# A hybrid transformer block with expert retrieval on one core: GpSimd builds the gated one-hots as outer products of two short factors, and 32 instead of 24 groups are scattered beside the routing

## What the block computes

```python
def peer_ffn(h, w_query, sub_keys, expert_u, expert_v):
    q = (x @ w_query).reshape(T, PEER_HEADS, 2, PEER_HALF)
    s1 = jnp.einsum('thd,kd->thk', q[:, :, 0], sk[0])
    s2 = jnp.einsum('thd,kd->thk', q[:, :, 1], sk[1])
    v1, i1 = lax.top_k(s1, PEER_TOPK)
    v2, i2 = lax.top_k(s2, PEER_TOPK)
    cand = (v1[..., :, None] + v2[..., None, :]).reshape(T, PEER_HEADS, PEER_TOPK * PEER_TOPK)
    sc, flat = lax.top_k(cand, PEER_TOPK)
    e = (jnp.take_along_axis(i1, flat // PEER_TOPK, axis=-1) * PEER_NKEYS
         + jnp.take_along_axis(i2, flat % PEER_TOPK, axis=-1))
    g = jax.nn.softmax(sc, axis=-1).astype(h.dtype)
    ...
        u = expert_u[ec]
        a = jax.nn.gelu(jnp.einsum('cd,chkd->chk', xc, u))
        return jnp.einsum('chk,chkd->cd', gc * a, expert_v[ec])
```

## Time and profile before

| | |
|---|---|
| median of 3 runs | 1539.96 us (1539.79 to 1540.7) |
| the profiled execution | 1540.05 us, of which 1538.0 us from the first to the last instruction |
| PE busy | 1454.6 us, 95% |
| DVE busy | 1324.1 us, 86% |
| ACT busy | 691.7 us, 45% |
| POOL busy | 787.6 us, 51% |
| PE on the chain that ended last | 75% (DVE 16%) |
| routing of tile 3 done, late rounds begin | about 541 us into the span |
| tile 1 begins on PE | 561.65 us |
| its store is issued | 605.49 us |
| last group, dense stage begins | about 631 us |

### The profile page before, as it was taken

One profiled execution on the slowest core, in us unless ns is written; L12 is line 12 of the kernel. 1 busy time (PEld: TensorE's weight loads), 2 busy tenths in 40 slices (PEclk: granted clock), 3 DMA queues, 4 the chain that ended last, 5 costly groups with the idle time before them and its releaser, 6 DMA issues.

```text
span 1538.0 us, 25458 instructions
## 1 busy us (share of the span) xinstructions
PE 1454.6 (95%) x7847; PEld 1247.5 (81%) x7847; DVE 1324.1 (86%) x2653; ACT 691.7 (45%) x1383; POOL 787.6 (51%) x733
## 2 busy tenths in 40 slices
PE   4999999999989868989999999999999999999996
PEld 3777677867678657779899989999999989999985
DVE  5877746246999989799899999999999999999998
ACT  5232456313157657634444444444444444444443
POOL 1010000000059957677777767667767767667662
PEclk8999999999999979999999999999999999999998
DMA  9895211350021165899999999999999999999994
GB/s 344 328 386 192 82 55 56 137 195 1 1 111 50 49 243 234 333 401 402 401 401 401 401 399 401 401 385 401 401 376 402 399 373 402 401 377 402 399 384 162
DMA packets 164992, 448.85 MB, mean 292 GB/s; under 512 B 14683, under 2 KB 50675, under 8 KB 164284
## 3 DMA queue, kind: packets, MB, share of 16 engines
q1 hardware_dynamic: 108732, 243.33, 42.5%
q0 software_dynamic: 56192, 204.66, 33.9%
HBM read 423.72 MB, written 22.32 MB: 290 GB/s over the span
## 4 chain that ended last, share of the span: by engine, by line
PE 75%; DVE 16%; issue 3%; DMA 2%; ACT 2%; POOL 1%; SPq 0%; ACTq 0%; DVEq 0%; POOLq 0%
PE bank L954 15%; PE bank L1217 8%; PE bank L1216 8%; PE bank L1215 8%; PE bank L1238 7%; PE bank L1239 7%; PE bank L1240 7%; PE bank L1231 4%; PE bank L1230 3%; PE bank L1137 2%; PE bank L1050 2%; DMA w_scratch<-staged 1%; PE bank L897 1%; DVE top_i L1951 1%; DVE scores L1952 1%
## 5 line engine op out<-in xcount | busy, mean ns | idle before, releaser
L790 POOL DMA_INDIRECT u_rows<-u_exp,small x192 | 260.0, 1354 | 92.0 <-POOL small L786 52.0
L790 POOL DMA_INDIRECT v_rows<-v_exp,small x192 | 258.9, 1348 | 91.3 <-POOL small L786 51.8
L1215 PE MATMUL bank<-h_hi,u_hi 128*128 128x320 f32 x944 | 291.2, 308 | 0.7 <-ACT staged L1513 0.7
L1217 PE MATMUL bank<-h_hi,u_lo 128*128 128x320 f32 x944 | 291.7, 309 | 0.0
L1216 PE MATMUL bank<-h_lo,u_hi 128*128 128x320 f32 x944 | 291.5, 309 | 0.0
L1238 PE MATMUL bank<-v_hi,g_parts 128*128 128x512 f32 x512 | 199.9, 391 | 0.0
L1239 PE MATMUL bank<-v_lo,g_parts 128*128 128x512 f32 x512 | 199.5, 390 | 0.0
L1240 PE MATMUL bank<-v_hi,g_parts 128*128 128x512 f32 x512 | 199.4, 390 | 0.0
L1616 ACT ACTIVATE v_hi<-v_raw 128x1024 fp32r<-128x1024 f32 x128 | 135.2, 1056 | 104.4 <-PE bank L1240 80.3
L1215 PEld LDWEIGHTS bank<-h_hi,u_hi 128*128 128x128 f32 x944 | 177.2, 188 | 5.4 <-ACT staged L1513 0.9
L1216 PEld LDWEIGHTS bank<-h_lo,u_hi 128*128 128x128 f32 x944 | 177.2, 188 | 4.6
(11 more groups left out here) (255 smaller groups left out, 2953.4 us busy)
## 6 DMA issues: line engine op xcount, KB each, us to landing
v_raw<-v_exp SPq DMA_DIRECT2D x128, 512.0 KB
u_raw<-u_by_key SPq DMA_DIRECT2D x120, 512.0 KB
ada_blk<-ada_w SPq DMA_DIRECT2D x22, 1024.0 KB, 10.9
ring<-w_in SPq DMA_DIRECT2D x18, 1024.0 KB, 10.0
w_row<-w_scratch SPq DMA_DIRECT2D x128, 128.0 KB
w_scratch<-staged SPq DMA_DIRECT2D x2, 4096.0 KB, 17.0
xr<-x SPq DMA_DIRECT2D x8, 512.0 KB, 6.4
ring<-w_branch SPq DMA_DIRECT2D x4, 1024.0 KB, 5.0
```

What stands on the lines that cost most here:

```text
L790: pool.indirect_dma_start(out=rows[s], out_offset=None, in_=table, in_offset=bass.IndirectOffsetOnAxis(ap=ix[:, s:s + 1], axis=0))\
L1215: pe.matmul(o, u_hi[:, r, k], h2_hi[:, k], start=(k == 0), stop=False)
L1217: last = pe.matmul(o, u_lo[:, r, k], h2_hi[:, k], start=False, stop=(k == KD - 1))
```

## The change

What it does:

- `gate_rows` on GpSimd no longer compares a row of 128 lanes with the key. A key j is split into a high part (a multiple of 8) and a low part 0 to 7, by adding and taking away a large number that rounds. `factors` makes a one-hot of 16 for the high part and a one-hot of 8 times the gate for the low part, for 16 tokens at once (early) or 6 (late). A row of `hot2` is their outer product, so one TENSOR_TENSOR writes the rows of a whole group. The factors lie in the new tile `hot_parts`.
- `EARLY` is 32 instead of 24: all groups of tile 0 run in the early way. In every fourth early group GpSimd makes `hot1` too, in two instructions, and ScalarE skips it. 48 late groups, 12 rounds, are left.
- `POOL_ROWS` is (2, 4, 0, 0): GpSimd makes 6 of the 16 late rows, VectorE 10.
- `h2_lo`, a subtraction over 128 x 2560, moves from VectorE to GpSimd, between the early groups and the late rounds. ScalarE's copy-outs of tile 1 wait for it, as before.
- `u_early` has 3 slots instead of 4 (`UNITS`), since `hot_parts` takes their room; SP's stores move a little. GpSimd's first early work waits for `x_saved`, because `hot_parts` lies in `xr`.
- `g_half_done` is folded into `g_hi_done`, with the same waits.

```diff
-EARLY = 24
+EARLY = NT * 8
+FOUR = 4
+EARLY_ACT = EARLY - EARLY // FOUR
-POOL_ROWS = (0, 2, 0, 1)
+POOL_ROWS = (2, 4, 0, 0)
+WIDE, FINE = 16, 8
+UNITS = 3
+ROUND = 1.5 * FINE * 2.0 ** 23
...
-            def gate_rows(n, g, to, token, some):
...
-                for j in some:
-                    ins = pool.tensor_scalar(to[:, j], lane, four[:, 0, j:j + 1], four[:, 1, j:j + 1],
-                                             ALU.is_equal, ALU.mult)
-                ins.then_inc(hot2_pool, 1)
+            def split_keys(n, token, w):
+                pool.tensor_copy(key_gate[:, :, 0:w], picksT[:, 1:3, at_w]).then_inc(hot_factors, 1)
+                pool.tensor_scalar(high, keys, -(FINE - 1) / 2, ROUND, ALU.add, ALU.add).then_inc(hot_factors, 1)
+                pool.tensor_scalar(high, high, -ROUND, 0.0, ALU.add, ALU.add).then_inc(hot_factors, 1)
+                pool.tensor_tensor(low, keys, high, ALU.subtract).then_inc(hot_factors, 1)
+            def factors(n, token, w):
+                split_keys(n, token, w)
+                pool.tensor_tensor(wide, lane[:, 0:P:FINE].unsqueeze(1).to_broadcast([P, w, WIDE]),
+                                   key_high[:, 0:w].unsqueeze(2).to_broadcast([P, w, WIDE]), ALU.subtract)
+                pool.tensor_tensor(fine, lane[:, 0:FINE].unsqueeze(1).to_broadcast([P, w, FINE]),
+                                   key_low[:, 0:w].unsqueeze(2).to_broadcast([P, w, FINE]), ALU.subtract)\
+                    .then_inc(hot_factors, 1)
+                pool.tensor_scalar(both, both, 0.0, 1.0, ALU.is_equal, ALU.mult).then_inc(hot_factors, 1)
+                pool.tensor_tensor(fine, fine, key_gate[:, 1, 0:w].unsqueeze(2).to_broadcast([P, w, FINE]), ALU.mult)\
+                    .then_inc(hot_factors, 1)
+            def gate_rows(freed, to, w, first, rows):
+                pool.tensor_tensor(to.rearrange("p j (a b) -> p j a b", b=FINE),
+                                   wide_of(w)[:, some].unsqueeze(3).to_broadcast(shape),
+                                   fine_of(w)[:, some].unsqueeze(2).to_broadcast(shape), ALU.mult).then_inc(hot2_pool, 1)
...
             for g in range(EARLY):
-                gate_rows(g, g, first_hot2[g % 2], 4 * g, range(4))
+                if g % FOUR == 0:
+                    if g:
+                        pool.wait_ge(hot2_pool, g)
+                    factors(7 * (g // FOUR), 4 * g, 4 * FOUR)
+                gate_rows(g - 1, first_hot2[g % 2], 4 * FOUR, g % FOUR * 4, 4)
+                if g % FOUR == 2:
+                    pool.wait_ge(w_full, g)
+                    ones = first_hot1[1]
+                    pool.tensor_tensor(ones, lane.unsqueeze(1).to_broadcast([P, 4, P]),
+                                       picksT[:, 0, 4 * g + 4:4 * g + 8].unsqueeze(2).to_broadcast([P, 4, P]),
+                                       ALU.subtract).then_inc(ones_differ, 1)
+                    pool.wait_ge(ones_differ, g // FOUR + 1)
+                    pool.tensor_scalar(ones, ones, 0.0, 1.0, ALU.is_equal, ALU.mult).then_inc(hot1_pool, 1)
+            pool.wait_ge(h2_hi_done, 1)
+            pool.tensor_tensor(h2_lo, h2T[:, :, 0:DS], h2_hi.bitcast(F32), ALU.subtract).then_inc(h2_lo_done, 1)
...
             def late_rows(lo, hi):
                 with pool.Fori(lo, hi) as m:
-                    for n in range(2):
-                        gate_rows(m * 2 + (EARLY // 2 + n), m * 4 + (2 * n + 1), hot2[2 * n + 1], m * 16 + (8 * n + 4),
-                                  range(4 - POOL_ROWS[2 * n + 1], 4))
+                    pool.wait_ge(hot2_pool, m * 2 + (EARLY - EARLY // 2))
+                    factors(m * 7 + 7 * (EARLY // FOUR - EARLY // 4), m * 16 + (4 - POOL_ROWS[0]), sum(POOL_ROWS))
+                    for r in range(2):
+                        gate_rows(m * 4 + (r - 3), hot2[r][:, 4 - POOL_ROWS[r]:4], sum(POOL_ROWS),
+                                  POOL_ROWS[0] * r, POOL_ROWS[r])
```

More of the change, by code:

```diff
@@ L391, in build @@
         x_back = at("x_back", 35.5, [P, NT, D])
-        u_early = [at(f"u_early{s}", 4 * s, [P, KD, P]) for s in range(4)]
+        u_early = [at(f"u_early{s}", 4 * s, [P, KD, P]) for s in range(UNITS)]
         a_out = [at(f"a_out{s}", 28 + 1.25 * s, [P, DS]) for s in range(3)]
@@ L672, in _ @@
             sp.wait_ge(h2_ready, NT)
-            for k in range(4):
+            for k in range(UNITS):
                 load_ahead(k)
-            for k in range(4):
-                load_ahead(4 + k)
+            for k in range(N_RUN - UNITS):
+                load_ahead(UNITS + k)
                 save_ahead(k)
-            for k in range(4, N_RUN):
+            for k in range(N_RUN - UNITS, N_RUN):
                 save_ahead(k)
-            sp.wait_ge(a_early_full, N_RUN)
-            sp.dma_start(h2T_kept, h2T[:, :, 0:DS]).then_inc(x_saved, 16)
+                if k == N_RUN - 2:
+                    sp.wait_ge(a_early_full, N_RUN)
+                    sp.dma_start(h2T_kept, h2T[:, :, 0:DS]).then_inc(x_saved, 16)
             sp.wait_ge(scores_read, NT)
@@ new lines, in gate_rows @@
+            def gate_rows(freed, to, w, first, rows):
+                if not isinstance(freed, int) or freed > 0:
+                    pool.wait_ge(w_full, freed)
+                    pool.nop().then_inc(pool_passed, 1)
+                some, shape = slice(first, first + rows), [P, rows, WIDE, FINE]
+                pool.tensor_tensor(to.rearrange("p j (a b) -> p j a b", b=FINE),
+                                   wide_of(w)[:, some].unsqueeze(3).to_broadcast(shape),
+                                   fine_of(w)[:, some].unsqueeze(2).to_broadcast(shape), ALU.mult).then_inc(hot2_pool, 1)
@@ L1148, in first_ahead @@
                 for d in (2 * part, 2 * part + 1):
-                    last = pe.matmul(o, u_early[k % 4][:, d], h2T[:, d, 0:DS], start=(d == 0), stop=(d == KD - 1))
+                    last = pe.matmul(o, u_early[k % UNITS][:, d], h2T[:, d, 0:DS], start=(d == 0), stop=(d == KD - 1))
                 if part == 3:
@@ L1193, in _ @@
             alone = min(BEGUN_WITH) // 4
-            with pe.Fori(EARLY // 4, DS_GROUPS // 4) as m:
-                four_groups(m)
             picks_across(2)
             stored(pe, ("kT", 2))
-            with pe.Fori(DS_GROUPS // 4, alone) as m:
+            with pe.Fori(EARLY // 4, alone) as m:
                 four_groups(m)
@@ L1641, in block_step @@
                 act.activation(g_hi(r), gated[:, r], ACT.Copy).then_inc(g_hi_done, 1)
-                act.activation(g_half(r), gated[:, r, DS - EX:DS], ACT.Copy).then_inc(g_half_done, 1)
+                act.activation(g_half(r), gated[:, r, DS - EX:DS], ACT.Copy).then_inc(g_hi_done, 1)
                 if not isinstance(b, int) or b + 1 < NK:
```

107 lines of the change are left out of this document (62 added, 45 removed).

## The result

The changed kernel takes 1588.13 us (median of four runs, 1585.22 to 1588.92), the kernel before 1539.88 us beside it: a ratio of 1.0306, 95% interval 1.0294 to 1.0318. The forecast was 1557, with a range of 1533 to 1573. The direction was right, the size was not: the time lies outside the range.

The account below looks back on a forecast made before the run. PE is busy almost throughout, so the scatter only moves the dense stage's begin, when tile 1 is complete. Tile 1 begins 6.6 us later and takes 10.6 longer: 17.2 on 1540.05 gives 1557 us, range 1533 to 1573.

Parts of the forecast that it names:

- the clock to watch: End of the scatter: the moment tile 1 is complete, 605.49 before, sets when the dense stage begins; forecast 17.2 us later.
- Two limits stand side by side: Late rounds: ACT with PE takes 5.23 us, VectorE 5.2, so taking rows off VectorE alone gives nothing.
- A product of 512, 1.11 us: Group product on GpSimd: 0.19 us start plus 0.92 for 512 elements, at 1.8 ns an element.
- dearer products: Rival, chance 0.22: GpSimd products cost 2.2 ns an element or more, late rounds 7.2 us, time 1566 and up.
- 448 with one 0.41: Early factors for 16 tokens on GpSimd: 448 one-input elements take 0.41 us of the 4.35 us total.
- A hot1: ... 0.47: GpSimd's hot1 in every fourth early group: 1.11 + 0.21 + 0.19 + 0.47 = 1.98 us.
- The bound at 4.7 ns: GpSimd products at the gated row's price: four groups some 23 us, a round 10.5, over 130 us slower.
- Products being plain: Reason given for keeping GpSimd products at 4.7 ns an element, over 130 us slower, out of the range.
- 2.0: Early stage: 2.0 us as PE's part in a four of 8.8 + 1.05 + 2.0 + 1.05 = 12.9 us.
- h2_lo, factors of the first round: GpSimd between early groups and late rounds: h2_lo 4.8 us, then factors for 6 tokens 3.5 us and a wait of 0.21.
- The late rounds: GpSimd becomes the bound: 5.5 us of its work plus 1.3 lost to VectorE, 6.8 a round, tile 1 plus 10.6.
- while VectorE lost nothing: Where VectorE's h_lo (2.82 us) met a GpSimd row, the row took 3.68 us instead of 0.79 and VectorE lost none.

Follow-up runs that it names:

- run 9: Kernel before the change with 3 of VectorE's 13 hot2 rows left out per late round from tile 1 on, last round excepted: 1540.30 us, ratio 0.9993.
- Run 4: Changed kernel with GpSimd's two comparisons as single operations (is_equal 0) instead of pairs (is_equal 0, times 1): 1578.04 us, ratio 1.0233.
- Run 1: Changed kernel with hot1 of all 32 early groups back on ScalarE, none on GpSimd: 1564.71 us, ratio 1.0162.
- run 7: Changed kernel with factors made ahead, every hot1 on ScalarE, h2_lo on VectorE behind its first late round, late rounds as before the change: 1540.29 us, ratio 0.9994.
- run 10: run 7 with h2_lo in front of VectorE's first late round instead of behind it: 1539.37 us, ratio 0.9986.
- run 8: run 7 with the early hot2 rows made by comparison with two pointers instead of factored products: 1547.08 us, ratio 1.0039.
- run 6: Changed kernel with the next four groups' factors made ahead and every hot1 on ScalarE: 1561.13 us, ratio 1.0134.
- run 5: Changed kernel with a second hot_parts, the next four groups' factors made between the third and fourth product: 1583.58 us, ratio 1.0279.

## Why the prediction was wrong in size

- **What bounds the kernel, and the clock to watch** ("tile 1 complete"): right. 44.8 of the 47.8 us stand at the issue of tile 1's store, and from there to the end of the span it is 932.5 us in the kernel before, 935.5 in the changed one and 933.0 to 937.9 in the experiments. The forecast had this stretch unchanged; it is 3.0 us longer.
- **"Two limits stand side by side"**: run 9 bears it out for the limit that is not VectorE's.
- **A product of 512, 1.11 us**: right (1.07), though the 1.8 ns behind it was low for the long subtraction: h2_lo took 5.58 us, 2.1 ns an element behind its start, not 4.8. The Trainium skill ("GPSIMD Engine Reference", section 3.1) gives about 2.6 cycles an element for an operation with two inputs, at 1.2 GHz an estimate of 2.2 ns. The row of h2_lo agrees; the product of 512, with (1.07 - 0.19) / 512 = 1.7 ns, is cheaper than that. The rival "dearer products" (2.2 ns or more, 1566 and up) contains the time, but its condition didn't hold for the products.
- **"448 with one 0.41" and "A hot1: ... 0.47"**: this step failed. I priced the comparisons by AFFINE_SELECT, 0.91 ns an element, since they have no pointers. They cost 3.4 ns ((1.51 - 0.19) / 384; (1.92 - 0.19) / 512), nearer to the gated row's 4.7, which is also a TENSOR_SCALAR that compares. By that a four has 1.0 us more in its factors and 1.3 in its hot1. The bound at 4.7 ns was kept out of the range by an argument on products alone ("Products being plain"); plain products with dear comparisons, which is what came, had no case. Run 4 shows that most of the price is not the second operation's.
- **"2.0" for PE's part of a four**: this failed too. I let PE run at the speed of an undisturbed stretch, and forecast waits for it in the same sentence. Behind the wait at 505.52 it ran at a granted clock of 0.54, 1.0 us more for the group and 1.6 for the block. So this four took 6.6 + 10.9 = 17.5 us, not 4.1 + 8.8 = 12.9: 2.1 us are GpSimd's (the comparisons, less a subtraction cheaper than forecast), 2.5 the clock. The division is shown for this four only, and the fours differ (14.3 to 19.9 us). Over the whole stage the forecast fell behind in steps: group 13, forecast for 502.0, came at 511.11 (9.1 late), group 29, forecast for 555.7, at 574.74 (19.0 late), and the last product ended at 581.1 instead of 558.8 (22.3 late). Run 1 takes the hot1 away and gives 22.8 us back, run 4 takes a fifth off the comparisons' length and gives 10, some of it in the late rounds; how the 22 us divide between price and clock stays open.
- **h2_lo, factors of the first round**: 5.58 + 4.2 us against 4.8 + 3.7, 1.3 us more. With the 22.3 this is the error at tile 1's begin, about 23.
- **The late rounds**: right in mechanism, 7.14 against 6.8 us. GpSimd's own part is 6.16 us instead of 5.5 (the comparison again: 0.71 for 144 elements instead of 0.32, and steps of 6 elements 0.25 to 0.29 instead of 0.19), the stops by VectorE 1.0 instead of 1.3. Eight rounds 0.34 us longer are 2.7 of the 4.3 us that tile 1 took beyond the forecast. The other 1.6 are a slip: 8 x 6.8 = 54.4 was set against a measured 43.84, which is eight rounds of 5.23 and 2.0 more.
- **"while VectorE lost nothing"**: wrong as a rule. It was true of the one meeting that I had read. It added nothing in the changed kernel. In run 7 it ends VectorE's routing 12.6 us later than rows do, and the expected gain is missing.
- Two sums of the prediction don't come out, without effect on the forecast: PE's other work over three groups with queries is 3 x 3.75 - 1.05 = 10.2, not 10.6, and a four of the dearer rival is 12.2, not 11.9.

What stays open is how the 20 us of longer busy time of PE split exactly over stages, and why kernels with products vary more (7 us over 11 times of run 7, 8 over 12 of run 10, 1.6 over 5 of run 8); that the meetings of GpSimd and VectorE fall differently each time is a guess.

## What to carry to other kernels

Price an instruction by a row of the same kind (a comparison by a comparison), however much its operands differ, and where two kinds of row are within reach, put both into the range. When lumpy work feeds a consumer through two slots, count all that the producer does between a slot's release and its refill: moving a piece helps where it is then alone in its interval (run 6 against run 1), and not where it joins another (run 5). And where a forecast contains a wait of TensorE, look for a row behind a wait of that length, and price by it what TensorE does next: here a group and a block took 2.5 us more behind 3.87 us of idle time.

## What the runs showed of the hardware that I had not expected

- GpSimd stops VectorE as VectorE stops GpSimd. Beside GpSimd's subtraction of 5.58 us, eight rows of VectorE, otherwise 0.26 us each, took 8.18 us in the changed kernel (VectorE, then GpSimd):

```profile
580.13 8.18 DVE L2169 TENSOR_SCALAR hot<-lane,picksT 128x128 f32<-128x128 f32 x8
```

```profile
581.09 5.58 POOL L883 TENSOR_TENSOR h_lo<-h2T,h_hi 128x2560 fp32r<-128x2560 f32 x1
```

  The Trainium skill ("SBUF — State Buffer", "Who interferes with whom") says that where an operation of VectorE needs the port pair that it shares with GpSimd, whichever starts first has the pair for its whole instruction. These rows agree, and so do run 6's. The two-pointer rows of run 8, which read memory too, are 0.79 us long and filled most of the time (GpSimd busy 92.28 of 100.35 us), left VectorE's routing as it was (540.94), which the rule alone doesn't tell.
- On GpSimd a comparison with constants costs 3.4 ns an element in its form with two operations, and 2.6 in that with one; with two tensors as inputs, the product of 512 costs 1.7 and the subtraction of 2560 costs 2.1.
